# Three running sums in place of one more pass: the norm ahead of the feed-forward in a one-step decoder layer

## What is computed

```python
def decoder_layer(x, c, ...):
    mod = (jax.nn.silu(c) @ w_ada + b_ada)[:, None, :]
    sh1, sc1, gt1, sh2, sc2, gt2 = jnp.split(mod, N_MOD, axis=-1)
    h = rmsnorm(x, g_pre_mix) * (1.0 + sc1) + sh1
    m, k_rows, v_rows, s_new = token_mixer(h, w_in, ...)       # ends with concat(o_sb, o_g) @ w_out
    x = x + gt1 * rmsnorm(m, g_post_mix)
    h = rmsnorm(x, g_pre_ffn) * (1.0 + sc2) + sh2
    f = (jax.nn.silu(h @ w_ffn_gate) * (h @ w_ffn_up)) @ w_ffn_down
    x = x + gt2 * rmsnorm(f, g_post_ffn)
```

## Time and profile before

| | us |
|---|---|
| median of 3 runs | 1504.8 (1504.07 to 1504.97) |
| span of the profiled execution | 1501.4 |
| PE busy | 1439.7 (96%) |
| DVE busy | 913.3 (61%) |
| ACT busy | 660.7 (44%) |
| chain that ended last: PE | 80% of the span |
| chain that ended last: DMA | 12% of the span |
| mean granted TensorE clock | 0.987 of 2.4 GHz |

### The profile page before, as it was taken

One profiled execution on the slowest core, in us unless ns is written; L12 is line 12 of the kernel. 1 busy time (PEld: TensorE's weight loads), 2 busy tenths in 40 slices (PEclk: granted clock), 3 DMA queues, 4 the chain that ended last, 5 costly groups with the idle time before them and its releaser, 6 DMA issues.

```text
span 1501.4 us, 29221 instructions
## 1 busy us (share of the span) xinstructions
PE 1439.7 (96%) x11274; PEld 1274.0 (85%) x11274; DVE 913.3 (61%) x1501; ACT 660.7 (44%) x1277; POOL 105.2 (7%) x205
## 2 busy tenths in 40 slices
PE   7779999998899999998999999999999999999997
PEld 2247787887568787796899999999999999999997
DVE  2243588995687666457657666566665665446444
ACT  1023477776655544336434434444344343334333
POOL 1000311112322200100000000000000000200000
PEclk9979999999899999999999999999999999999999
DMA  9999999999999978996766565665656555855552
GB/s 370 421 362 360 389 387 402 369 333 397 385 373 326 338 259 281 393 328 257 264 184 182 168 193 172 184 179 168 194 177 185 177 171 186 235 182 181 178 179 94
DMA packets 139043, 396.56 MB, mean 264 GB/s; under 512 B 13130, under 2 KB 17393, under 8 KB 126145
## 3 DMA queue, kind: packets, MB, share of 16 engines
q1 hardware_dynamic: 117730, 319.39, 62.9%
q0 software_dynamic: 21232, 76.10, 13.4%
HBM read 382.14 MB, written 11.21 MB: 262 GB/s over the span
## 4 chain that ended last, share of the span: by engine, by line
PE 80%; DMA 12%; DVE 3%; ACT 2%; issue 1%; POOLq 0%; SPq 0%; POOL 0%; DVEq 0%; ACTq 0%
PE ps L1907 23%; PE ps L1908 23%; PE ps L1909 23%; PE ps L1841 4%; DMA ada_s<-in_w_ada 3%; DMA raw<-in_w_in 2%; DMA v_page<-in_cache_v 2%; DMA k_page<-in_cache_k 2%; DMA ada_r<-in_w_ada 2%; PE ps L2039 2%; DMA x_keep<-x_t 1%; PE ps L1965 1%; DVE k_page L1275 1%; DMA k_page<-in_cache_v 1%; PE ps L1884 1%
## 5 line engine op out<-in xcount | busy, mean ns | idle before, releaser
L1907 PE MATMUL ps<-h_hi,w_hi 128*128 128x264 f32 x2304 | 665.7, 289 | 7.6 <-DVE h_lo L1213 3.6
L1908 PE MATMUL ps<-h_lo,w_hi 128*128 128x264 f32 x2304 | 656.5, 285 | 0.0
L1909 PE MATMUL ps<-h_hi,w_lo 128*128 128x264 f32 x2304 | 655.9, 285 | 0.0
L1907 PEld LDWEIGHTS ps<-h_hi,w_hi 128*128 128x128 f32 x2304 | 435.9, 189 | 53.4 <-issue 38.3
L1729 DVE TENSOR_TENSOR w_lo<-raw,w_hi 128x1024 fp32r<-128x1024 f32 x256 | 309.5, 1213 | 275.4 <-ACT w_hi L1018 274.1
L1018 ACT ACTIVATE w_hi<-raw 128x1024 fp32r<-128x1024 f32 x264 | 278.4, 1059 | 405.0 <-PE ps L1909 393.9
L1908 PEld LDWEIGHTS ps<-h_lo,w_hi 128*128 128x128 f32 x2304 | 435.3, 189 | 0.1
L1909 PEld LDWEIGHTS ps<-h_hi,w_lo 128*128 128x128 f32 x2304 | 434.2, 188 | 0.0
L1225 DVE TENSOR_TENSOR w_lo<-raw,w_hi 128x1024 fp32r<-128x1024 f32 x136 | 166.2, 1223 | 162.4 <-ACT w_hi L702 155.1
L702 ACT ACTIVATE w_hi<-raw 128x1024 fp32r<-128x1024 f32 x128 | 134.9, 1055 | 193.4 <-PE ps L1909 162.4
L1908 PE MATMUL ps<-act_lo,w_hi 128*128 (+1 forms) x704 | 200.4, 285 | 0.0
(11 more groups left out here) (336 smaller groups left out, 1211.6 us busy)
## 6 DMA issues: line engine op xcount, KB each, us to landing
ada_r<-in_w_ada SPq DMA_DIRECT2D x64, 1024.0 KB, 9.4
raw<-in_w_in SPq DMA_DIRECT2D x96, 512.0 KB, 8.3
raw<-in_w_ffn_gate SPq DMA_DIRECT2D x88, 512.0 KB, 3.7
raw<-in_w_ffn_up SPq DMA_DIRECT2D x88, 512.0 KB, 3.8
raw<-in_w_ffn_down SPq DMA_DIRECT2D x88, 512.0 KB, 4.1
ada_s<-in_w_ada SPq DMA_DIRECT2D x32, 1024.0 KB, 13.2
k_page<-in_cache_k POOLq DMA_DIRECT2D x64, 512.0 KB, 7.5
v_page<-in_cache_v POOLq DMA_DIRECT2D x38, 512.0 KB, 7.7
```

The costliest lines, as they stand in the source:

```text
L1907: mm(out, w_hi, xh, start=first, stop=False)
L1908: mm(out, w_hi, xl, start=False, stop=False)
L1909: return mm(out, w_lo, xh, start=False, stop=last)
```

## The change

By |m g + x|^2 = |x|^2 + 2 r (x, g m) + r^2 |g m|^2, with r the rstd of the mix and g m its gated form, the second sum of squares no longer needs the new x. Three sums are gathered during the output projection, all in `squares`: of the mix's squares (tiles 0 to 3), of gated mix times old x (8 to 11, slots of `XG_AT`), and of the gated mix's squares (12 to 15, formed by ACT, added in the slots of `GG_AT`). Each is folded to one tile in slots 124 to 126. |x|^2 itself is copied from the first norm's PSUM bank to `x_sq_sum` (`SXX`), written to HBM behind x_keep and read back behind x_old.

For the last group the terms are made bank by bank; PE makes two products with ones for the first sum and three for each of the others, into banks 5 and 7. The new x is made pair by pair: pair 0 right after the first rstd, pair p + 1 ahead of `pair_low(p)`. The FFN's `lo(2)` to `lo(9)` move into the pair loop, ACT's `hi(p + 3)` too. In the gap PE now does ada step 48, the six products, and steps 49 to 55; step 56 + u stands behind FFN unit u, and 61, 62, 63 together behind unit 5. Some semaphores are shared; nothing waits otherwise for that.

```diff
+        GGT = put("gg_part", [P, MT, T], at=at_pv)
+        R2 = put("rstd_ffn", [P, T], at=r0 + 98432)
+        SXX = put("x_sq_sum", [P, T], at=r0 + 99680)
...
+        XG_AT = {110: 0, 115: 1, 123: 2}
+        GG_AT = {117: 1, 125: 2}
+        M_LAST, X_LAST, G_LAST = (1, 2, 3, 9), (4, 5, 6, 7), (10, 11, 13, 14)
...
             sp.dma_start(x_keep, X[:, :, :]).then_inc(x_moved, 16)
+            sp.wait_ge(x_dve, KC // 2 + 1)
+            sp.dma_start(sxx_keep, SXX[:, :]).then_inc(x_moved, 16)
...
-                    sp.wait_ge(x_moved, 16)
+                    sp.wait_ge(x_moved, 32)
...
                     sp.dma_start(XOLD[:, :, :], x_keep).then_inc(x_moved, 16)
+                    sp.dma_start(SXX[:, :], sxx_keep).then_inc(x_moved, 16)
...
+            def gg_squares(gi):
+                act.wait_ge(gm_ready, gi + 1)
+                if gi == 2:
+                    act.wait_ge(acc_ready, 1)
+                c = MT * gi
+                s.activation(SQD[:, 12:16, :] if gi == 0 else GGT[:, :, :], MT_[:, c:c + MT, :], ACT.Square).then_inc(gg_sq, 1)
...
+            def last_square(m):
+                act.wait_ge(gm_ready, NOUT + 2 * m)
+                s.activation(SQD[:, G_LAST[m], :], MT_[:, KC - MT + m, :], ACT.Square).then_inc(gg_sq, 1)
+
+            act.wait_ge(acc_ready, 4)
+            act.wait_ge(scl_ready, 1)
             for m in range(MT):
                 if m < 3:
                     act.wait_ge(bank_done, 3 * (NIN + NOUT - 1) + m + 1)
                 else:
                     act.wait_ge(unit_used, W_FFN)
-                s.activation(SQD[:, KC - MT + m, :], ps[:, m, 0:T], ACT.Square).then_inc(last_sq, 1)
-                act.wait_ge(scl_ready, 1)
+                s.activation(SQD[:, M_LAST[m], :], ps[:, m, 0:T], ACT.Square).then_inc(last_sq, 1)
                 s.activation(MT_[:, KC - MT + m, 0:TP], ps[:, m, 0:TP], ACT.Copy,
                              scale=scale_t[:, KC - MT + m, 0:1]).then_inc(bank_out, 1)
+                if m in (1, 2):
+                    last_square(m - 1)
 
             rs_sum(6, 5, 2)
-            for u in range(2, 4):
-                hi_n(W_FFN, u)
-
-            def x_scale(q):
+            last_square(2)
+            last_square(3)
+            hi_n(W_FFN, 2)
+
+            def x_scale(p):
 
                 act.wait_ge(scl_ready, 2)
-                for k in range(4 * q, 4 * q + 4):
+                act.wait_ge(x_new, p + 1)
+                for k in (2 * p, 2 * p + 1):
                     ins = s.activation(F_LO[:, k, 0:TP], X[:, k, 0:TP], ACT.Identity, scale=scale_t[:, k, 0:1])
                 ins.then_inc(x_scaled, 1)
 
-            for i, (k0, k1) in enumerate(PIECES):
-                act.wait_ge(x_new, i + 1)
-                s.activation(SQD[:, k0:k1, :], X[:, k0:k1, :], ACT.Square).then_inc(sq_ready, 1)
-                if i < 2:
-                    x_scale(i)
-            rs_sum(7, 6, 3)
+            act.wait_ge(norm_rs, 4)
+            s.activation(R2[:, :], SXX[:, :], ACT.Ln, scale=1.0 / D, bias=eps_t[:, 0:1]).then_inc(rs_ready, 1)
+            act.wait_ge(rs_ready, 11)
+            s.activation(R2[:, :], R2[:, :], ACT.Exp, scale=-0.5).then_inc(rs_ready, 1)
+            x_scale(0)
+            hi_n(W_FFN, 3)
 
...
-                if p in (1, 2):
+                if p < UPC - 1:
                     x_scale(p + 1)
-                if 3 <= p:
-                    hi_n(W_FFN, p + 1)
+                if 1 <= p:
+                    hi_n(W_FFN, p + 3)
             mod_row(5)
-            for u in range(UPC + 1, UPC + 3):
-                hi_n(W_FFN, u)
...
+            v.tensor_copy(SXX[:, :], ps[:, 6, 0:T]).then_inc(x_dve, 1)
...
                 if st - 1 in MIX_AT:
                     c = MT * MIX_AT[st - 1]
-                    link(gated(MT_, c, c + MT))
+                    gated(MT_, c, c + MT).then_inc(gm_ready, 1)
+                    dve.wait_ge(gm_ready, MIX_AT[st - 1] + 1)
                     if c:
-                        link(v.tensor_tensor(SQD[:, 0:MT, :], SQD[:, 0:MT, :], SQD[:, c:c + MT, :], ALU.add))
-                if st == 123:
-                    fold(SQD, MT)
+                        link(v.tensor_tensor(SQD[:, 0:4, :], SQD[:, 0:4, :], SQD[:, 4:8, :], ALU.add))
+                if st in XG_AT:
+                    c = MT * XG_AT[st]
+                    if c == 0:
+                        dve.wait_ge(x_moved, 64)
+                    link(v.tensor_tensor(SQD[:, 4:8, :] if c else SQD[:, 8:12, :], MT_[:, c:c + MT, :], XOLD[:, c:c + MT, :],
+                                         ALU.mult))
+                    if c:
+                        link(v.tensor_tensor(SQD[:, 8:12, :], SQD[:, 8:12, :], SQD[:, 4:8, :], ALU.add))
+                if st in GG_AT:
+                    dve.wait_ge(gg_sq, GG_AT[st] + 1)
+                    v.tensor_tensor(SQD[:, 12:16, :], SQD[:, 12:16, :], GGT[:, :, :], ALU.add).then_inc(acc_ready, 1)
+                if st == 124:
+                    fold(SQD[:, 0:4, :], MT, sq_ready)
+                if st == 125:
+                    fold(SQD[:, 8:12, :], MT, acc_ready)
+                if st == 126:
+                    dve.wait_ge(acc_ready, 2)
+                    fold(SQD[:, 12:16, :], MT, acc_ready)
...
-            for m in range(MT - 1):
-                dve.wait_ge(last_sq, m + 1)
-                ins = v.tensor_tensor(SQD[:, 0, :], SQD[:, 0, :], SQD[:, KC - MT + m, :], ALU.add)
-                if m < MT - 2:
-                    link(ins)
-            ins.then_inc(sq_ready, 1)
-            dve.wait_ge(bank_out, MT * (NIN + NOUT))
-            link(v.tensor_tensor(MT_[:, KC - MT:KC, TP:T], ps[:, 0:MT, TP:T], scale_t[:, KC - MT:KC, 1:NC], ALU.mult))
+            dve.wait_ge(sq_ready, 5)
+            for m in range(MT):
+                k = KC - MT + m
+                if m < MT - 1:
+                    dve.wait_ge(last_sq, m + 1)
+                    ins = v.tensor_tensor(SQD[:, 0, :], SQD[:, 0, :], SQD[:, M_LAST[m], :], ALU.add)
+                    if m < MT - 2:
+                        link(ins)
+                    else:
+                        ins.then_inc(sq_ready, 1)
+                dve.wait_ge(bank_out, MT * (NIN + NOUT - 1) + m + 1)
+                v.tensor_tensor(MT_[:, k, TP:T], ps[:, m, TP:T], scale_t[:, k, 1:NC], ALU.mult).then_inc(gm_ready, 1)
+                dve.wait_ge(gm_ready, NOUT + 2 * m)
+                v.tensor_tensor(SQD[:, X_LAST[m], :], MT_[:, k, :], XOLD[:, k, :], ALU.mult).then_inc(gm_ready, 1)
+                if m < 2:
+                    dve.wait_ge(acc_ready, 4)
+                    dve.wait_ge(gm_ready, NOUT + 2 * m + 1)
+                    ins = v.tensor_tensor(SQD[:, 8, :], SQD[:, 8, :], SQD[:, X_LAST[m], :], ALU.add)
+                    if m == 0:
+                        link(ins)
+                    else:
+                        ins.then_inc(acc_ready, 1)
+                if m in (1, 2):
+                    dve.wait_ge(gg_sq, NOUT - 1 + m)
+                    ins = v.tensor_tensor(SQD[:, 12, :], SQD[:, 12, :], SQD[:, G_LAST[m - 1], :], ALU.add)
+                    if m == 1:
+                        link(ins)
+                    else:
+                        ins.then_inc(acc_ready, 1)
...
             dve.wait_ge(sums_done, 2)
             rstd_of(rstd[:, :], rvar[:, :], ps[:, 6, 0:T], D, 5, behind=True)
-            dve.wait_ge(x_moved, 32)
-            for i, (k0, k1) in enumerate(PIECES):
-                cs = slice(k0, k1)
-                link(v.tensor_tensor(MT_[:, cs, :], MT_[:, cs, :], rstd[:, :].unsqueeze(1).to_broadcast([P, k1 - k0, T]),
+            dve.wait_ge(sums_done, 3)
+            link(v.tensor_tensor(rvar[:, :], rstd[:, :], ps[:, 7, 0:T], ALU.mult))
+            link(v.scalar_tensor_tensor(rvar[:, :], ps[:, 5, 0:T], 2.0, rvar[:, :], ALU.mult, ALU.add))
+            link(v.tensor_tensor(rvar[:, :], rvar[:, :], rstd[:, :], ALU.mult))
+            v.tensor_tensor(SXX[:, :], SXX[:, :], rvar[:, :], ALU.add).then_inc(norm_rs, 1)
+
+            def pair_new(p):
+                cs = slice(2 * p, 2 * p + 2)
+                link(v.tensor_tensor(MT_[:, cs, 0:TP], MT_[:, cs, 0:TP], rstd[:, 0:TP].unsqueeze(1).to_broadcast([P, 2, TP]),
                                      ALU.mult))
-                v.tensor_tensor(X[:, cs, :], MT_[:, cs, :], XOLD[:, cs, :], ALU.add).then_inc(x_new, 1)
-            dve.wait_ge(x_new, len(PIECES))
+                v.tensor_tensor(X[:, cs, 0:TP], MT_[:, cs, 0:TP], XOLD[:, cs, 0:TP], ALU.add).then_inc(x_new, 1)
+
+            pair_new(0)
+            link(v.tensor_tensor(MT_[:, :, TP:T], MT_[:, :, TP:T], rstd[:, TP:T].unsqueeze(1).to_broadcast([P, KC, TS]), ALU.mult))
+            v.tensor_tensor(X[:, :, TP:T], MT_[:, :, TP:T], XOLD[:, :, TP:T], ALU.add).then_inc(hs_ready, 1)
+            dve.wait_ge(norm_rs, 4)
+            rstd_of(R2[:, :], rvar[:, :], SXX[:, :], D, 6)
             dve.wait_ge(scl_ready, 2)
+            dve.wait_ge(hs_ready, 1)
```

(54 more changed lines are left out.)

54 lines of the change are left out of this document (28 added, 26 removed).

## The result

Time after: 1508.6 us, median of 20 runs (1504.05 to 1511.38), against 1504.45 (20 runs) before. The ratio is 1.0028, with a 95% interval of 1.0021 to 1.0035: some 4.2 us slower. Both kernels' sets of runs are over 7 us wide, so it is only the medians of many runs that tell them apart. The profiled execution took 1506.4 us between its first and last instruction.

The account below looks back on a forecast made before the run. It took the norm's chain to bound the gap, DMA close behind: 1501.4 (profiled span) + 0.5 (sxx_keep) + 2.1 (loads and copy) = 1504.0, plus 3.4 to the median, 1507.4 us. Bounds 1504.9 to 1508.8; range with rivals 1504.3 to 1510.3.

Parts of the forecast that it names:

- DVE's third add: Last column group: DVE's third add into the first sum ends at 690.6 us, where before it was 687.0.
- The norm's chain: Between output projection and FFN: h_lo done at 705.15 instead of 709.38, so the first FFN unit could start 4.2 us earlier.
- The loads: Ada load 54 issued at 696.45, load 63 landing at 733.4; PE waits some 2.6 us, unit 6 starts at 734.5.
- the slower of the two paces: Weight load 4's landing to ada load 63's: 23.7 us for 8.5 MiB, against 21.1 at the first stretch's pace.
- The copy: ACT's mod_row(5) behind hi(10), after FFN unit 6: PE waits 1.8 us (1.6 to 2.0) before its transposes.
- sxx_keep: Early DMA behind x_keep, both awaited by SP: adds 0.5 us, range 0.3 to 1.2, reaching the end.
- The clock: Rival, chance 0.18: PE's clock falls behind the idle hole after 687.8, load 54 leaves 1.7 to 3.6 later; 1510 us.
- its own sign: Stated ground for being wrong: PE's clock falls between 688 and 710 us.
- the likeliest case: The forecast itself, chance 0.57: loads and copy start unit 7 2.1 us later, sxx_keep adds 0.5; 1507.4 us.
- the head start: First FFN unit 4.2 us earlier through the shorter norm work, gone by unit 6 because the loads set it.

Follow-up runs that it names:

- e4: Changed kernel in which SP no longer waits for sxx_keep ahead of ada loads 2 and 3 and the next weight load; ratio to the kernel before 1.0026.
- e3: Changed kernel with 14 products of ones with ones in PE's idle hole ahead of the first sum, no ada step moved; ratio to the kernel before 1.0025.
- e7: Kernel before with one move: ACT's copy mod_row(5) stands behind the high parts of units 9 and 10; ratio to the kernel before 1.0013.
- e2: Changed kernel with ada steps 48 to 50 in PE's idle hole ahead of the first sum, 51 to 55 behind the six sums; ratio to the kernel before 1.0016.
- e10: Changed kernel with ada steps 48 to 50 in PE's hole and 14 products of ones behind step 55; ratio to the kernel before 0.9987.
- e5: Changed kernel with DVE's three adds into the first sum ahead of its work for the other two sums; ratio to the kernel before 1.0027.
- e9: Changed kernel with DVE's first-sum adds first and ada steps 49 and 50 ahead of the six late-sum products; ratio to the kernel before 1.0001.
- a2: The changed kernel itself, unaltered, profiled and timed a second time; ratio to the kernel before 1.0030.
- e1: Changed kernel with ACT's copy mod_row(5) ahead of its high part of unit 10 instead of behind it; ratio to the kernel before 1.0031.

## Why the prediction was right, and where it was not

By its own steps, all behind L (the prediction's 687.5):

- **DVE's third add.** Forecast 3.1, measured 691.75 - 688.64 = 3.1. The 10.5 us of adds and folds ahead, and the 3.65 between the adds, were as laid out.
- **The norm's chain.** Forecast 705.15 - 687.5 = 17.65 to the first FFN product. In e4, whose clock stayed up, it is 17.78, in the two profiles of the changed kernel 19.97 and 20.19. The sum of durations held; the clock was the miss.
- **The loads.** The forecast let load 54 go out at 8.95 and load 63 land 36.95 later, at 45.9. Where the clock stayed up behind the hole (e3, e4) they did so at 9.2 and at 45.9. In six profiles in which load 54 left late (8.4 to 11.9) it was 36.5 to 36.8 from the one to the other, so the slower of the two paces I had, the one I took, was the right one. Where it left early (1.9 to 3.5, the kernel before and e7 included) it was 39.0 to 39.8. There load 53 goes out only 0.9 us ahead of load 54's issue and lands 4.1 to 5.7 us behind it, so most of that MiB crosses the DMA in the same time. In the changed kernel it landed 0.9 behind it. The DMA's share (the number before the last) is full either way, in the changed kernel and in e2:

```profile
699.50:736.20 36.70, 33.72 (x248) 22.04 (x240) 33.59 (x58) 22.17 (x42) 0.00 (x0) 0.91 0.99 395
```

```profile
689.00:728.80 39.80, 34.53 (x242) 24.20 (x235) 37.23 (x71) 23.32 (x46) 0.00 (x0) 0.91 0.99 390
```

PE's wait for load 63 was 2.15 in e4 (forecast 2.6) and 0.17 in the changed kernel's first profile, because PE itself was 2.2 late.
- **The copy.** Forecast 1.8, measured 1.69 as a wait and 1.93 in the step from unit 6 to unit 7.
- **sxx_keep.** Taken at 0.5 of a range to 1.2: SP's issue moved by 1.06 in the changed kernel and by 0.2 to 1.1 in the nine profiles with the wait, so the size was about right, but at most 0.3 us of it reached PE. "The chain goes straight through it, so what is added here reaches the end" was wrong, as the row of a chain shows who came last and not how much slack lies behind; in the changed kernel's chain x_keep does not appear at all. The Trainium skill (DMA: Bandwidth & Descriptors, Anatomy of one DMA), with its 2.0 us of fixed cost for a DMA, a fit made for DMAs that GpSimd issues, would have given the prediction's 2.3; the issues here moved by 1.1 at most, so the trace does not agree for a transfer queued behind another, as the prediction had it.
- **The clock,** the step that failed. It was a rival with 0.18; the forecast said that the clock stays up, "the idle time is a little shorter than the 3.24 of 370". The 3.24 is what a window of 3.40 us leaves beside its busy time; PE's wait there, as its timeline has it, was 3.56. The new one was 3.16, for the 2.85 laid out, and three of four profiles fell. By its own sign ("if PE's clock falls between 688 and 710") the prediction was wrong: it fell twice, to 0.54 and 0.52. The rival's price was partly right: load 54 left 1.95 later than forecast, inside its 1.7 to 3.6. What neither had is that in e4, where the clock stayed up behind the hole, it fell in the wait for load 63 and cost as much. Three profiles give 53.8 to 53.9 both ways, where the forecast has 50.05 + 2.1 = 52.2. In e3, where it fell nowhere, unit 7 came at 52.26 and PE waited 1.78 for load 63: without the clock the forecast's stage stands as laid out. The missing 1.7 us, and nothing for sxx_keep instead of 0.5, turn the forecast's +2.6 into a stage of +3.8; the measured +4.2 has an interval of 3.2 to 5.3.

So the likeliest case had the right mechanism for the head start, the loads and the copy, and lacked the clock. That the time fell inside its own bounds is in part luck. As changes against the 1504.8 it started from they are +0.1 to +4.0, the clock rival's +4.3 to +6.2; the measured +4.2 lies between the two. It is inside 1508.8 because the kernel before measured 1504.45 over 20 runs, 0.35 less than over the first three. The loads and the copy alone were given -0.2 to +2.8, and the stage is +3.8.

## What to carry to other kernels

When a change makes an engine idle ahead of its work, ask what that engine's finished steps release: here 9 us in the issue of one load were 5.9 us in the landing of the last, and moving three steps that were due anyway into the hole gave more (3.3 us at unit 7) than shortening the chain did (2.55). An idle stretch of TensorE of about 3 us may cost its clock or not, from one execution to the next, so one profile doesn't price it; fill it with work that is due, or with products of nothing. That pays in full (2.2 us in e10) where no transfer is waited for behind it. Two transfers that count on one semaphore have no landings of their own in the trace. And a copy that the tensor engine waits for belongs ahead of any conversion that itself waits for the tensor engine.

## What the runs showed of the hardware

Behind the same 3.16 us of idle time (3.17 in e4), with the same code around it, the clock fell to half in three profiles and stayed full in one; behind 3.18 and 3.19 us near 400 us it fell in e10 and not in e2. Waits of 2.15, 2.12 and 1.78 us for load 63 were followed by half clock in the first (e4) and by full clock in the others (e5, e3). Shorter waits in a row can be followed by it too: 1.42, 1.40 and 1.84 us with steps of 1.06 between them (e9), then 5.57 for a unit with its step of 4.12; with the first two of them alone (1.4 to 1.7 us each) the clock fell in the changed kernel, a2 and e1, and stayed up in e3, e4 and e5. With fourteen products of 128 columns in a wait the granted clock was 1.00 in the whole stage in all three kernels that have them; e2, which is e10 without them, fell to 0.59. (e5, without any, was at 1.00 as well.) After the fall over the first FFN unit the clock stood at 0.52 over 7.0 us in the changed kernel while PE was busy for 5.86 of them; in e9 the unit lost 1.45 us and in e2 2.36. And with a transfer of 0.135 MB issued 0.64 us behind one of 2.2 MB, the next issue, which waits for both, came 14.56 to 15.30 us behind the first one's in nine profiles, for 14.24 and 14.37 in the two kernels without the small one; it was 14.76 in e4, which does not wait for it.
